# Filler products in the expert stream, a split last load, and a reordered final normalization

## The chip, the cores and the metric

One core of one Trainium2 chip runs the whole program. The metric is the device time of one execution in microseconds; the number for a kernel is the median of several executions. All data is float32.

## What is computed

A transformer block and, behind it, a hybrid layer with a mixture of experts, over 256 tokens of width 1024. The stretch that the change touches is the mixture of experts and the last normalization:

```python
def hier_moe(h, w_group, b_group, w_expert, b_expert, w1, w3, w2):
    ...                                   # each of 256 tokens picks 2 of 32 experts
    def expert_block(args):
        xb, e = args
        hid = jax.nn.silu(xb @ w1[e]) * (xb @ w3[e])
        return hid @ w2[e]
    ...                                   # gated sum back to the tokens

x = x + hier_moe(rms_norm(x, g_ffn), ...)
return rms_norm(x, g_final)               # x * rsqrt(mean(x*x) + eps) * g
```

w1 and w3 are 1024 x 512 and w2 is 512 x 1024 for each of the 32 experts: 2 MiB each, 192 MiB in all.

## The kernel before

The queues of the five engines are written out by hand, with semaphores between them. The dense layers come first (to about 630 us); their weights pass through a ring of three slots and are split into two parts for products in higher precision. Then the experts follow one after another, in quads of four (QUAD = 4). Each expert has 32 slots (SLOTS); products use 32-column tiles of the array, four side by side.

**TensorE**, `quad_body(q)` from L1293: products that gather the quad's tokens (L1305, into banks 4 and 5); then for each expert e: wait for w1, 32 products (L1361, n = 0, into bank 6, columns 0 to 127), wait for w3, 32 products (L1361, n = 1, columns 128 to 255); for e = 0 the gates (`spread_gates`, L1329), else the previous expert's result is added to the tokens' sums (`add_to_tokens`, L1345, banks 0 to 3); wait for w2 and for the turned hidden values, 16 products (L1377, into bank 7, columns 0 to 255). A float32 product shows as two records of stationary load and two of matmul. Quads 0 and 1 are written out (`looped` is false); quads 2 to 7 are one hardware loop (L1387). `keep_warm(n, bank)` (L1058) makes n products of a 128 x 128 tile of ones whose result nobody reads; before, it is used in the program's first microseconds only.

**SyncE** (SP) issues all loads of expert weights. Buffers: `even_w`, `odd_w`, and for the first experts `third_w` and `fourth_w`. `stream(pass_, lo_pair)` (L781) runs over pairs of experts: for each of the three matrices it waits until the matrix of two experts earlier has been used (semaphores e_w1, e_up, e_y) and starts the load (L717), which raises landed_w[parity][which] by 16. Experts 8 to 31 come from this loop. Behind it, four stores of the output, 128 tokens x 512 columns each (L798 to L801); each waits for ScalarE (fin_act) or VectorE (fin_dve).

**ScalarE** applies silu (L1694) and copies an expert's result from bank 7 to `y_part` (L1699); at the end it squares and sums three of the four pieces of the output (L1710) and scales two by the inverse root (L1718).

**VectorE** multiplies silu by the up product (L2336) and turns it (L2341). At the end: a copy and a square sum of the fourth piece (L2366, L2368); `last_mean(tb)` for a block of 128 tokens (L2373 to L2375); two pieces times the gain (L2382); two pieces times inverse root and gain (L2388). **GpSimd** raises the mean to the power -0.5 for block 1, then block 0 (L872).

If more than 32 tokens choose one expert, further passes repeat the stream; with these inputs there is one pass (32 executions of L1694).

Of the kernel before, what the change touches and what calls it, by code (L numbers as in the profile page):

```python
# [31 lines left out]
P = 128  # L32
# [9 lines left out]
UC = 256  # L42
# [6 lines left out]
EXPERTS = GROUPS * PER_GROUP  # L49
# [3 lines left out]
QUAD = 4  # L53
# [236 lines left out]
def layers_kernel(nc, a, table, windows, out):  # L290
# [41 lines left out]
    ones = ones_r[:, :].bitcast(F32)  # L332
# [125 lines left out]
    ps = nc.alloc_psum_tensor("ps", [P, 8, 512], F32)  # L458
# [39 lines left out]
    def sem(name):  # L498
        return nc.alloc_semaphore(name)
# [52 lines left out]
    hot_ready, xg_done, xg_ready, gt_done, gt_ready = (sem(n) for n in ("hot_ready", "xg_done", "xg_ready",  # L552
                                                                        "gt_done", "gt_ready"))
    e_w1, e_w1_half = sem("e_w1"), sem("e_w1_half")
    e_up, e_silu, e_hid, e_hidT, e_y, e_yA = (sem(n) for n in (
        "e_up", "e_silu", "e_hid", "e_hidT", "e_y", "e_y_act"))
    gt_rest, xg_half = sem("gt_rest"), sem("xg_half")
# [111 lines left out]
    def _(sp):  # L669
# [45 lines left out]
        def expert_load(e, places, which, landing):  # L715
            src = sources[which][:, bass.ds(e, 1), :, :].rearrange("p e c n -> p (e c) n")
            sp.dma_start(places[which], src).then_inc(landing, 16)  # L717
# [60 lines left out]
            sp.wait_ge((e_w1, e_up, e_y)[which], 6)  # L778
            expert_load(7, odd_w, which, landed_w[1][which])

        def stream(pass_, lo_pair):  # L781

            with sp.Fori(lo_pair, EXPERTS // 2) as i:
                for odd in range(2):
                    e = sp.snap(i * 2 + odd)
                    used = sp.snap(i * 2 + (pass_ * EXPERTS + odd - 1))
                    for which in range(3):
                        sp.wait_ge((e_w1, e_up, e_y)[which], used)
                        expert_load(e, (even_w, odd_w)[odd], which, landed_w[odd][which])

        stream(0, 4)
        sp.wait_ge(passes_ready, 1)
        n_pass = sp.value_load(passes_i[0:1, 0:1], min_val=1, max_val=T // SLOTS)
        with sp.If(n_pass > 1):
            with sp.Fori(1, n_pass) as again:
                stream(again, 0)
            sp.nop()
        for tb, i in ((1, 0), (1, 1), (0, 0), (0, 1)):  # L798
            sp.wait_ge((fin_act, fin_dve)[i], 2 - tb)
            cols = slice(512 * i, 512 * i + 512)  # L800
            sp.dma_start(out[0, P * tb:P * tb + P, cols], n3[:, tb, cols]).then_inc(fin_out, 16)  # L801
# [75 lines left out]
    def _(pe):  # L877
# [177 lines left out]
                last = mm(ps[:, (6, 6, 7, 2)[n], P * tb:P * tb + P], scale, ident, start=True, stop=True)  # L1055
            last.then_inc(row_done, 1)

        def keep_warm(n, bank):  # L1058

            for _ in range(n):  # L1060
                mm(ps[:, bank, 0:P], ones, ones, start=True, stop=True)

        def turn_block(src, g, tb, n=None):

# [112 lines left out]
        for step, *arg in plan:  # L1177
# [110 lines left out]
           stop=False)  # L1288
# [4 lines left out]
        def quad_body(q):  # L1293

            looped = not isinstance(q, int)
            e0 = pe.snap(q * QUAD) if looped else q * QUAD

            if not looped:
                pe.wait_ge(n3_ready, 2)
            for half in range(2):  # L1300
                for tb in range(TB):
                    if half == 0:
                        pe.wait_ge(hot_part, q * 2 + (tb + 1))
                    for i in range(4):
                        last = mm(ps[:, 4 + half, P * i:P * i + P], n3g[:, tb, 4 * half + i, :], one_hot[:, tb, :],  # L1305
                                  start=tb == 0 and i == 0, stop=tb == 1 and i == 3)
                if half == 0:
                    last.then_inc(xg_half, 1)
            last.then_inc(xg_done, 1)

            def place_of(e):

                if looped:
                    arrived = pe.snap(q * 32 + 8 * (e - 2 + e % 2)) if e % 2 == 0 else pe.snap(q * 32 + 8 * (e - 1))
                    return (even_w, odd_w)[e % 2], landed_w[e % 2], arrived
                if q == 0:
                    return ((even_w, odd_w, third_w, fourth_w)[e],
                            (landed_w[0], landed_w[1], in_third3, in_fourth)[e], 16)
                return ((even_w, odd_w, third_w, odd_w)[e],
                        (landed_w[0], landed_w[1], in_third3, landed_w[1])[e], (32, 32, 32, 48)[e])  # L1320

            def spread_gates():

                pe.wait_ge(hot_ready, q + 1)
                for e in range(QUAD):
                    for tb in range(TB):
                        at_e = T * (e % 2) + P * tb
                        for g in range(4):
                            last = mm(ps[SLOTS * g:SLOTS * g + SLOTS, 4 + e // 2, at_e:at_e + P],  # L1329
                                      gated_hot[:, tb, SLOTS * e:SLOTS * e + SLOTS], ident, start=True, stop=True,  # L1330
                                      tile_position=(0, SLOTS * g))
                last.then_inc(gt_done, 1)

            def add_to_tokens(e):

                if e == 0:
                    pe.wait_ge(gt_ready, q + 1)
                    pe.wait_ge(gt_rest, q + 1)
                    if not looped and q == 0:
                        pe.wait_ge(seeded, 4)  # L1340
                pe.wait_ge(e_yA, pe.snap(e0 + (e + 1)) if looped else e0 + e + 1)
                for tb in range(TB):
                    for g in range(4):
                        part = slice(SLOTS * g, SLOTS * g + SLOTS)
                        last = mm(ps[:, g, T * tb:T * tb + T], gate_T[part, e, P * tb:P * tb + P],  # L1345
                                  y_part[part, e % 2, :], start=False, stop=True, tile_position=(SLOTS * g, 0),
                                  skip_group_check=True)
                last.then_inc(comb_done, 1)

            for e in range(QUAD):  # L1350
                places, landing, arrived = place_of(e)
                done = pe.snap(e0 + e) if looped else e0 + e
                for n in range(2):
                    if not looped and e == 0 and (q == 0 or n == 0):
                        pe.wait_ge(first_half[n], 16 * (q + 1))
                    pe.wait_ge(landing[n], arrived)
                    for c in range(KC):
                        if e == 0 and n == 0 and c % 4 == 0:
                            pe.wait_ge((xg_part, xg_ready)[c // 4], q + 1)
                        for g in range(4):  # L1360
                            last = mm(ps[SLOTS * g:SLOTS * g + SLOTS, 6, P * n:P * n + P],  # L1361
                                      xg[:, c, SLOTS * e:SLOTS * e + SLOTS], places[n][:, c, P * g:P * g + P],
                                      start=c == 0, stop=c == KC - 1, tile_position=(0, SLOTS * g))
                        if not looped and q == 0 and e == 0 and n == 0 and c == KC // 2 - 1:
                            last.then_inc(e_w1_half, 1)
                    last.then_inc((e_w1, e_up)[n], 1)
                if e == 0:
                    spread_gates()
                else:
                    add_to_tokens(e - 1)  # L1370
                if not looped and q == 0 and e == 0:
                    pe.wait_ge(first_half[2], 16)
                pe.wait_ge(landing[2], arrived)
                pe.wait_ge(e_hidT, done + 1)
                for b in range(4):
                    for g in range(4):
                        last = mm(ps[SLOTS * g:SLOTS * g + SLOTS, 7, 0:UC],  # L1377
                                  hid_T[:, SLOTS * b:SLOTS * b + SLOTS], places[2][:, b, UC * g:UC * g + UC],
                                  start=b == 0, stop=b == 3, tile_position=(0, SLOTS * g))
                last.then_inc(e_y, 1)  # L1380
            add_to_tokens(QUAD - 1)
# [340 lines left out]
    def _(dve):  # L1722
# [636 lines left out]
        def piece_of(tb, i):  # L2359

            cols = slice(512 * i, 512 * i + 512)
            return (n3[:, tb, cols].rearrange("p (a b) -> p a b", a=2), ps[:, 2 * i:2 * i + 2, T * tb:T * tb + T],
                    gain_rows[1][:, cols].rearrange("p (a b) -> p a b", a=2))
# [7 lines left out]
        def last_mean(tb):  # L2371

            link(v.tensor_reduce(stat[:, last_event, tb:tb + 1], sq_part[:, tb, 0:2], AX.X, ALU.add))  # L2373
            v.tensor_scalar(stat[:, last_event, 2 + tb:3 + tb], stat[:, last_event, tb:tb + 1], 1.0 / D, EPS, ALU.mult,
                            ALU.add).then_inc(mean_last, 1)  # L2375
# [2 lines left out]
        last_mean(1)  # L2378
        dve.wait_ge(sq_last, 2)
        for tb in (1, 0):  # L2380
            dst, src, gain = piece_of(tb, 0)
            v.tensor_tensor(dst, src, gain, ALU.mult).then_inc(fin_gain, 1)  # L2382
        dve.wait_ge(sq_last, 3)
        last_mean(0)
        for n, tb in enumerate((1, 0)):
            dst, src, gain = piece_of(tb, 1)
            dve.wait_ge(root_last, n + 1)
# [29 lines left out]
```

## Time and profile before

| | |
|---|---|
| median of 3 executions | 1073.48 us (1072.98 to 1074.26) |
| profiled execution, device time | 1076.11 us |
| its span, first to last instruction | 1073.7 us |
| TensorE busy | 932.4 us (87%) |
| VectorE, ScalarE, GpSimd busy | 505.3, 364.0, 29.5 us |
| DMA moved | 310.00 MB, 289 GB/s over the span |
| chain that ended last | TensorE 61%, DMA 34% |

```profile
PE 932.4 (87%) x9984; PEld 767.4 (71%) x9984; DVE 505.3 (47%) x815; ACT 364.0 (34%) x517; POOL 29.5 (3%) x35
```

Busy time is time in which an engine executes; a span is cut into 40 slices on the page, each with the busy share in tenths, the granted clock of TensorE (PEclk; 9 stands for 0.9 or more of 2.4 GHz) and the share of the 16 DMA engines. PE is TensorE's matmuls, PEld its loads of the stationary operand. Behind an instruction stands the idle time before it, and what ended it; "issue" means that the profile shows nothing that was waited for.

### The profile page before, as it was taken

What the parts mean: (1) busy time and instruction counts of PE and PEld (TensorE: products, weight loads), DVE (VectorE), ACT (ScalarE), POOL (GpSimd) and SP (SyncE); (2) the same over time, 40 slices, a digit from 0 to 9 for tenths busy, and PEclk for the clock granted to TensorE, in tenths of its full rate; (3) what the DMA queues carried; (4) which work ended last, traced back from release to release, by engine and by line L of the source; (5) the groups of instructions that cost most, each with busy time, mean ns of one, the idle gap of its engine ahead of it and who ended that gap; (6) DMA issues with size and microseconds to landing.
All of it is one profiled execution on the core that took longest, in us unless ns stands there. A gap on an engine that the chain in (4) does not pass through costs nothing.

```text
span 1073.7 us, 22635 instructions
## 1 busy us (share of the span) xinstructions
PE 932.4 (87%) x9984; PEld 767.4 (71%) x9984; DVE 505.3 (47%) x815; ACT 364.0 (34%) x517; POOL 29.5 (3%) x35
## 2 busy tenths in 40 slices
PE   9999999999999999999999998976766667575764
PEld 8998877888888888988777886754545545364642
DVE  5647768687676668889877651110000101010101
ACT  6445766454444345444666330110000000000001
POOL 0200002110000000000000000000000000000000
PEclk9999999999999999999999999998888889889887
DMA  9954434545554644444457999999999999999994
GB/s 329 312 178 164 152 130 162 172 162 196 195 185 169 214 156 158 158 157 160 156 192 285 397 397 425 419 427 426 427 428 428 428 428 429 428 427 428 429 428 205
DMA packets 86830, 310.00 MB, mean 289 GB/s; under 512 B 5612, under 2 KB 46264, under 8 KB 73976
## 3 DMA queue, kind: packets, MB, share of 16 engines
q1 hardware_dynamic: 85104, 304.72, 72.8%
q0 software_dynamic: 1056, 4.20, 1.2%
q8 instruction: 42, 0.69, 0.3%
q10 hardware_dynamic: 616, 0.28, 0.1%
q14 instruction: 12, 0.10, 0.0%
HBM read 308.15 MB, written 1.05 MB: 288 GB/s over the span
## 4 chain that ended last, share of the span: by engine, by line
PE 61%; DMA 34%; DVE 2%; issue 1%; ACT 1%; POOL 1%; POOLq 0%; SPq 0%; DVEq 0%; ACTq 0%
DMA arena<-in_w 33%; PE ps L882 13%; PE ps L884 12%; PE ps L883 12%; PE ps L1006 7%; PE ps L1377 4%; PE ps L1008 4%; PE ps L1361 2%; DMA arena<-in_w_in 1%; PE ps L1155 1%; PE ps L1143 1%; PE ps L1305 1%; POOL stat L816 0%; PE ps L1067 0%; PE ps L981 0%
## 5 line engine op out<-in xcount | busy, mean ns | idle before, releaser
L1361 PE MATMUL ps<-arena,xg 128*32 128x128 f32 x2816 | 110.7, 322 | 73.6 <-DMA arena<-in_w 72.5
L1747 DVE TENSOR_TENSOR w_split<-arena,w_split 128x2048 fp32r<-128x2048 f32 (+1 forms) x69 | 157.2, 2288 | 29.1 <-ACT w_split L1422 28.6
L2336 DVE TENSOR_TENSOR hid<-silu_e,ps 128x128 f32<-128x128 f32 x32 | 12.1, 378 | 318.5 <-ACT silu_e L1694 318.5
L1361 PEld LDWEIGHTS ps<-arena,xg 128*32 128x32 f32 x2816 | 94.7, 130 | 93.1 <-DMA arena<-in_w 87.2
L1422 ACT ACTIVATE w_split<-arena 128x2048 fp32r<-128x2048 f32 x70 | 132.8, 1900 | 67.7 <-PE ps L884 57.8
L1006 PE MATMUL ps<-x_both,w_split 128*128 128x512 f32 x352 | 124.5, 398 | 0.0
L882 PE MATMUL ps<-w_split,x_both 128*128 128x512 f32 x256 | 102.0, 398 | 0.0
L883 PE MATMUL ps<-w_split,x_both 128*128 128x512 f32 x256 | 99.8, 390 | 0.0
L884 PE MATMUL ps<-w_split,x_both 128*128 128x512 f32 x256 | 99.8, 390 | 0.0
L1008 PE MATMUL ps<-x_both,w_split 128*128 128x256 f32 x352 | 98.6, 280 | 0.0
L1377 PE MATMUL ps<-arena,hid_T 128*32 128x256 f32 x960 | 67.3, 425 | 28.7 <-DMA arena<-in_w 28.1
L1694 ACT ACTIVATE silu_e<-ps 128x128 f32<-128x128 f32 x32 | 8.9, 277 | 243.0 <-PE ps L1361 243.0
L1006 PEld LDWEIGHTS ps<-x_both,w_split 128*128 128x128 f32 x352 | 66.1, 188 | 16.3 <-issue 0.3
L882 PE MATMUL ps<-x_both,w_split 128*128 128x256 f32 (+1 forms) x256 | 72.8, 285 | 0.9 <-ACT p_tok L1450 0.9
L1377 PEld LDWEIGHTS ps<-arena,hid_T 128*32 128x32 f32 x960 | 32.2, 118 | 57.5 <-issue 35.7
L884 PE MATMUL ps<-x_both,w_split 128*128 128x256 f32 (+1 forms) x256 | 72.3, 283 | 0.0
L883 PE MATMUL ps<-x_both,w_split 128*128 128x256 f32 (+1 forms) x256 | 72.3, 282 | 0.0
L882 PE MATMUL ps<-w_split,o_hi 128*128 128x512 f32 (+1 forms) x176 | 68.2, 388 | 0.5 <-DVE gates L1968 0.5
L1757 DVE TENSOR_TENSOR w_split<-arena,w_split 128x2048 fp32r<-128x2048 f32 x24 | 55.0, 2293 | 26.3 <-ACT w_split L1432 25.0
L884 PE MATMUL ps<-w_split,o_lo 128*128 128x512 f32 (+1 forms) x176 | 67.1, 381 | 0.0
L883 PE MATMUL ps<-w_split,o_hi 128*128 128x512 f32 (+1 forms) x176 | 66.9, 380 | 0.0
L1008 PEld LDWEIGHTS ps<-x_both,w_split 128*128 128x128 f32 x352 | 66.4, 189 | 0.3
(328 smaller groups left out, 1470.5 us busy)
## 6 DMA issues: line engine op xcount, KB each, us to landing
arena<-in_w SPq DMA_DIRECT2D x71, 2048.0 KB, 26.2
arena<-in_w_in SPq DMA_DIRECT2D x41, 1024.0 KB, 5.0
even_w<-in_w SPq DMA_DIRECT2D x13, 2048.0 KB, 27.3
arena<-in_w_ffn_in SPq DMA_DIRECT2D x22, 1024.0 KB, 5.1
third_w<-in_w SPq DMA_DIRECT2D x6, 2048.0 KB, 16.1
arena<-in_w_ffn_out SPq DMA_DIRECT2D x11, 1024.0 KB, 4.8
arena<-in_w_out SPq DMA_DIRECT2D x8, 1024.0 KB, 6.1
arena<-in_w SPq DMA_DIRECT2D x6, 1024.0 KB, 6.4
```

The costliest lines, as they stand in the source:

```text
L882: mm(dst, l_hi, r_hi, start=start, stop=False)
L883: mm(dst, l_hi, r_lo, start=False, stop=False)
L884: return mm(dst, l_lo, r_hi, start=False, stop=stop)
L1006: mm(ps[:, bank + n, :], hi[:, c, col], x_both[:, c, :, :].rearrange("p a b -> p (a b)"), start=c == 0, stop=False)
L1008: last = mm(ps[:, bank + n, 0:T], lo[:, c, col], x_hi[:, c, :], start=False, stop=c == kc - 1)
L1143: last = nc.tensor.transpose(m[:, P * t:P * t + P], src[:, P * t:P * t + P], ident)
L1361: last = mm(ps[SLOTS * g:SLOTS * g + SLOTS, 6, P * n:P * n + P], xg[:, c, SLOTS * e:SLOTS * e + SLOTS], places[n][:, c, P * g:P * g + P], ...
L1377: last = mm(ps[SLOTS * g:SLOTS * g + SLOTS, 7, 0:UC], hid_T[:, SLOTS * b:SLOTS * b + SLOTS], places[2][:, b, UC * g:UC * g + UC], start=b ...
L1422: fn(w_hi[:, u % 3, 0:n], ring[:, u % 3, 0:n], ACT.Copy).then_inc(hi_ready, 1)
L1747: v.tensor_tensor(w_lo[:, u % 3, 0:n], ring[:, u % 3, 0:n], w_hi[:, u % 3, 0:n].bitcast(F32), ALU.subtract).then_inc(lo_ready, 1)
L1757: v.tensor_tensor(w_lo[:, s, :], ring[:, s, :], w_hi[:, s, :].bitcast(F32), ALU.subtract)\
L2336: v.tensor_tensor(hid[:, :].rearrange("p (b i) -> p i b", b=4), silu_e[:, :].rearrange("p (i b) -> p i b", b=4), ps[:, 6, P:2 * P].rearran ...
```

## The change

- TensorE: in looped quads, five products of ones ahead of the wait for w1 and five ahead of the wait for w3 (bank 6, columns 256 to 383), three ahead of the wait for w2 (bank 7, the same columns). `keep_warm` takes a column for that.
- SyncE: the stream's loop runs over quads instead of pairs and stops before the last quad, which is written out. The last expert's w2 is loaded by two transfers: rows 0 to 2 of each partition's four (12 KB), which raise landed_w, and row 3 (4 KB), which raises the new semaphore last_block. Each quad of the loop raises last_block by 16 as well.
- TensorE: in each looped quad, before the last quarter (b = 3) of the last expert's down products, a wait for last_block against q * 16 - 16.
- VectorE: the mean of block 0 is computed between the two scalings by the gain instead of behind both.
- SyncE: the stores go in the order block 1 first half, block 0 first half, block 1 second half, block 0 second half.

```diff
--- before.py
+++ after.py
@@ -552,6 +552,7 @@
     hot_ready, xg_done, xg_ready, gt_done, gt_ready = (sem(n) for n in ("hot_ready", "xg_done", "xg_ready",
                                                                         "gt_done", "gt_ready"))
     e_w1, e_w1_half = sem("e_w1"), sem("e_w1_half")
+    last_block = sem("last_block_w2_in")
     e_up, e_silu, e_hid, e_hidT, e_y, e_yA = (sem(n) for n in (
         "e_up", "e_silu", "e_hid", "e_hidT", "e_y", "e_y_act"))
     gt_rest, xg_half = sem("gt_rest"), sem("xg_half")
@@ -778,24 +779,34 @@
             sp.wait_ge((e_w1, e_up, e_y)[which], 6)
             expert_load(7, odd_w, which, landed_w[1][which])
 
-        def stream(pass_, lo_pair):
-
-            with sp.Fori(lo_pair, EXPERTS // 2) as i:
-                for odd in range(2):
-                    e = sp.snap(i * 2 + odd)
-                    used = sp.snap(i * 2 + (pass_ * EXPERTS + odd - 1))
-                    for which in range(3):
-                        sp.wait_ge((e_w1, e_up, e_y)[which], used)
-                        expert_load(e, (even_w, odd_w)[odd], which, landed_w[odd][which])
-
-        stream(0, 4)
+        def stream(pass_, lo_quad):
+
+            def load_expert(e, j, used):
+
+                for which in range(3):
+                    sp.wait_ge((e_w1, e_up, e_y)[which], used)
+                    if isinstance(e, int) and (j, which) == (QUAD - 1, 2):
+                        for rows_, landing in ((slice(0, 3), landed_w[1][2]), (slice(3, 4), last_block)):
+                            sp.dma_start(odd_w[2][:, rows_, :], sources[2][:, e, rows_, :]).then_inc(landing, 16)
+                    else:
+                        expert_load(e, (even_w, odd_w)[j % 2], which, landed_w[j % 2][which])
+
+            with sp.Fori(lo_quad, EXPERTS // QUAD - 1) as i:
+                for j in range(QUAD):
+                    load_expert(sp.snap(i * QUAD + j), j, sp.snap(i * QUAD + (pass_ * EXPERTS + j - 1)))
+                sp.nop().then_inc(last_block, 16)
+            for j in range(QUAD):
+                e = EXPERTS - QUAD + j
+                load_expert(e, j, sp.snap(pass_ * EXPERTS + (e - 1)) if not isinstance(pass_, int) else e - 1)
+
+        stream(0, 2)
         sp.wait_ge(passes_ready, 1)
         n_pass = sp.value_load(passes_i[0:1, 0:1], min_val=1, max_val=T // SLOTS)
         with sp.If(n_pass > 1):
             with sp.Fori(1, n_pass) as again:
                 stream(again, 0)
             sp.nop()
-        for tb, i in ((1, 0), (1, 1), (0, 0), (0, 1)):
+        for tb, i in ((1, 0), (0, 0), (1, 1), (0, 1)):
             sp.wait_ge((fin_act, fin_dve)[i], 2 - tb)
             cols = slice(512 * i, 512 * i + 512)
             sp.dma_start(out[0, P * tb:P * tb + P, cols], n3[:, tb, cols]).then_inc(fin_out, 16)
@@ -1055,10 +1066,10 @@
                 last = mm(ps[:, (6, 6, 7, 2)[n], P * tb:P * tb + P], scale, ident, start=True, stop=True)
             last.then_inc(row_done, 1)
 
-        def keep_warm(n, bank):
+        def keep_warm(n, bank, col=0):
 
             for _ in range(n):
-                mm(ps[:, bank, 0:P], ones, ones, start=True, stop=True)
+                mm(ps[:, bank, col:col + P], ones, ones, start=True, stop=True)
 
         def turn_block(src, g, tb, n=None):
 
@@ -1353,6 +1364,8 @@
                 for n in range(2):
                     if not looped and e == 0 and (q == 0 or n == 0):
                         pe.wait_ge(first_half[n], 16 * (q + 1))
+                    if looped:
+                        keep_warm(5, 6, UC)
                     pe.wait_ge(landing[n], arrived)
                     for c in range(KC):
                         if e == 0 and n == 0 and c % 4 == 0:
@@ -1370,9 +1383,13 @@
                     add_to_tokens(e - 1)
                 if not looped and q == 0 and e == 0:
                     pe.wait_ge(first_half[2], 16)
+                if looped:
+                    keep_warm(3, 7, UC)
                 pe.wait_ge(landing[2], arrived)
                 pe.wait_ge(e_hidT, done + 1)
                 for b in range(4):
+                    if looped and (e, b) == (QUAD - 1, 3):
+                        pe.wait_ge(last_block, pe.snap(q * 16 - 16))
                     for g in range(4):
                         last = mm(ps[SLOTS * g:SLOTS * g + SLOTS, 7, 0:UC],
                                   hid_T[:, SLOTS * b:SLOTS * b + SLOTS], places[2][:, b, UC * g:UC * g + UC],
@@ -2378,10 +2395,11 @@
         last_mean(1)
         dve.wait_ge(sq_last, 2)
         for tb in (1, 0):
+            if not tb:
+                dve.wait_ge(sq_last, 3)
+                last_mean(0)
             dst, src, gain = piece_of(tb, 0)
             v.tensor_tensor(dst, src, gain, ALU.mult).then_inc(fin_gain, 1)
-        dve.wait_ge(sq_last, 3)
-        last_mean(0)
         for n, tb in enumerate((1, 0)):
             dst, src, gain = piece_of(tb, 1)
             dve.wait_ge(root_last, n + 1)
```

## Rows read from the trace of the kernel before

**Rows 1.** The page: span, and granted clock and DMA share in 40 slices.
```profile
span 1073.7 us, 22635 instructions
...
PEclk9999999999999999999999999998888889889887
DMA  9954434545554644444457999999999999999994
```

**Rows 2.** DMA queues and issues, 770 to 1064 us: packets, MB, share; KB each, us to landing.
```profile
q1 hardware_dynamic: 8462, 123.11, 98.4%
issues: line engine op xcount, KB each, median us to landing
arena<-in_w SPq DMA_DIRECT2D x46, 2048.0 KB, 27.2
```

**Rows 3.** Timeline of TensorE, down products of experts 9 to 11: start, us, count, idle before.
```profile
736.39 3.40 PE L1377 MATMUL ps<-arena,hid_T 128*32 128x256 f32 x32 [1.94 <-DMA arena<-in_w]
751.08 1.93 PE L1377 MATMUL ps<-arena,hid_T 128*32 128x256 f32 x32 [0.32 <-DMA arena<-in_w]
...
766.89 3.20 PE L1377 MATMUL ps<-arena,hid_T 128*32 128x256 f32 x32 [1.94 <-DMA arena<-in_w]
```

**Rows 4.** Timeline of the last expert on TensorE.
```profile
1050.71 3.60 PE L1361 MATMUL ps<-arena,xg 128*32 128x128 f32 x64 [2.90 <-DMA arena<-in_w]
...
1055.60 1.95 PE L1361 MATMUL ps<-arena,xg 128*32 128x128 f32 x64 [1.29 <-DMA arena<-in_w]
...
1057.48 1.15 PE L1345 MATMUL ps<-y_part,gate_T 32*128 32x256 f32 x16
...
1060.53 3.28 PE L1377 MATMUL ps<-arena,hid_T 128*32 128x256 f32 x32 [1.90 <-DMA arena<-in_w]
```

**Rows 5.** Stretches: length, busy us (records) of PE, PEld, DVE, ACT, POOL, clock, DMA, GB/s.
```profile
1056.00:1057.00 1.00, 1.00 (x48) 1.00 (x40) 0.00 (x0) 0.00 (x0) 0.00 (x0) 1.00 0.69 295
1057.00:1058.00 1.00, 1.00 (x29) 0.79 (x24) 0.07 (x1) 0.28 (x1) 0.00 (x0) 1.00 0.42 180
...
1059.00:1060.00 1.00, 0.00 (x0) 0.00 (x0) 0.00 (x0) 0.00 (x0) 0.00 (x0) 1.00 0.08 33
```

**Rows 6.** Timeline of TensorE, 0 to 40 us, the products of ones.
```profile
1.07 4.21 PE L1061 MATMUL ps<-ones 128*128 128x128 f32 x18 [1.07 <-DVE ones L2074]
...
6.72 1.95 PE L1061 MATMUL ps<-ones 128*128 128x128 f32 x16
```

**Rows 7.** Timeline of the end, VectorE and GpSimd.
```profile
1067.24 1.28 DVE L2382 TENSOR_TENSOR n<-ps,gain_row 128x512 f32<-128x512 f32 x2
1067.42 0.57 POOL L872 TENSOR_TENSOR stat<-stat,minus_half 128x1 f32<-128x1 f32 x1 [402.38 <-DVE stat L2374]
...
1068.62 0.15 DVE L2374 TENSOR_SCALAR stat<-stat 128x1 f32<-128x1 f32 x1
1068.69 0.74 DVE L2388 SCALAR_TENSOR_TENSOR n<-n,stat,gain_row 128x512 f32<-128x512 f32 x1
...
1068.85 1.00 POOL L872 TENSOR_TENSOR stat<-stat,minus_half 128x1 f32<-128x1 f32 x1 [0.86 <-DVE stat L2374]
...
1069.88 0.75 DVE L2388 SCALAR_TENSOR_TENSOR n<-ps,stat,gain_row 128x512 f32<-128x512 f32 x1 [0.45 <-POOL stat L872]
```

**Rows 8.** Timeline of SyncE, the last two stores of the output.
```profile
1070.63 0.33 SPq L801 DMA_DIRECT2D out<-n  x1
...
1071.01 0.43 SPq L801 DMA_DIRECT2D out<-n  x1
```

**Rows 9.** Stretches as in rows 5: between two stalls, loop start to a stall, one quad.
```profile
649.25:655.26 6.01, 5.38 (x128) 4.09 (x127) 0.00 (x0) 0.39 (x1) 0.00 (x0) 1.00 1.02 431
710.17:720.40 10.23, 8.54 (x191) 7.84 (x188) 1.38 (x3) 0.87 (x2) 0.00 (x0) 1.00 1.01 426
771.75:829.15 57.40, 38.26 (x804) 29.51 (x800) 5.21 (x14) 3.83 (x10) 0.00 (x0) 0.88 1.01 428
```

**Rows 10.** DMA queue of instruction fetches, 640 to 702 us, then 709 to 770 us.
```profile
q8 instruction: 10, 0.16, 1.0%
...
q8 instruction: 7, 0.11, 0.8%
```

## The prediction

> **What bounds the kernel now.** I began with the page's slices: from about 590 us on the DMA row stands at 9 in every slice to the last, while PEclk drops below full speed [rows 1]. Next the DMA view of 770 to 1064 us: 2048 KB loads alone, each landing some 27 us after its issue [rows 2]. Down products that wait for a load start 14.69 us apart (736.39, 751.08) [rows 3], which is three loads, so a load takes 4.90 us and more than five are in flight. TensorE is idle in between; what it wins inside the stream is worth nothing. Only three things count: when the last bytes land, what follows them, and anything else that uses the 16 DMA engines.
>
> At the end, expert 31's up matrix is used from 1055.60, its last down matrix from 1060.53, after 1.90 us of idleness [rows 4]. The DMA share falls from 0.69 over 0.42 to 0.08 in 1056 to 1060 [rows 5]: the engines end one after another, and the slowest sets the landing. Behind it stands a serial chain to the end.
>
> **Part 1: last down matrix in two transfers, dummies ahead.** The profiled run computed this matrix in 3.28 us [rows 4]; the same 32 records take 1.93 us at 2.4 GHz (751.08), 3.40 at nearly 1.2 GHz throughout [rows 3].
> - Transfer: three quarters of the bytes land a quarter of 4.90 us, 1.22 us, earlier. Bounds: nothing earlier (if both completions come together) to 1.22. I take 1.2; the quarters queue behind each other on the same engines. A second set of packet starts I take as 0.1 us at most.
> - Dummies: 18 records ran in 4.21 us cold, 16 in 1.95 us warm [rows 6]. One dummy is two records, so 0.24 us warm, 0.47 cold: five are 1.2 or 2.3 us, three 0.7 or 1.4 us. In the stream they lie in idle time of 2.90 us (1050.71) and 1.90 us (1060.53) [rows 4]; where a quad begins they make TensorE some 1 us late, which the 27 us of loads in flight cover [rows 2]. If that cover were gone, each would cost its own time.
> - Clock: the longest regular idle stretch shrinks from 2.90 to 1.7 us. Since the up products and additions (1055.60 to 1058.63) are followed directly by dummies, I expect 2.4 GHz at the last matrix.
> - New end: additions end 1058.63 [rows 4], three dummies to 1059.37, just behind the first landing. Three quarters of 1.93 us to 1060.82; the last quarter has landed at about 1060.6, its products take 0.48: 1061.30, against 1060.53 + 3.28 = 1063.81. **-2.5 us**; if cold in spite of the dummies, 1063.4 (-0.4). Against an execution whose last matrix ran warm already (end 1062.46) it is only -1.2.
>
> **Part 2: the mean ahead of the second scaling, stores.** Before: two scalings from 1067.24, 0.60 us apart, then the mean (ends 1068.77), then the second power 1068.85 to 1069.85, then the last products at 1069.88 [rows 7]. After: scaling one, mean from 1067.84 to about 1068.2, scaling two beside the power. The first power took 0.57, the second 1.00 us, beside L2388, which reads two SBUF tensors [rows 7]. Moved, the power runs beside L2382, which reads one from PSUM; I take 0.57, so the root is there at 1068.85. L2388 then runs back to back (1068.69, 1069.43) and ends at 1070.2 instead of 1070.63. The store of block 0's first half goes at about 1069.7, and the other two follow 0.38 us apart, the spacing of the last two now (1070.63, 1071.01) [rows 8]: the last at 1070.45 instead of 1071.01. **-0.6 us**, 0 to -0.6. If the power stays at 1.00 the gain is about 0.2. The Trainium skill, SBUF — State Buffer, section Who interferes with whom, says that a VectorE instruction with two SBUF inputs contends with a GpSimd instruction that reads SBUF; by it the 0.57 stands, and the two rows agree.
>
> The nops and the unrolled last quad on SP, and the wait on last_block, cost 0: SP only has to issue within those 27 us. Behind that wait are the 8 last records alone, which need these bytes anyway.
>
> **Part 3: what else the dummies bring, code.** Each dummy is 4 instructions (two loads of the stationary operand, two products), 52 per quad: 208. A quad of the loop now has 804 + 800 records, with branches and register work about 1612 [rows 9]. Instruction fetches are packets of 16 KB: 10 are 0.16 MB, and 7 fell in the first looped quad, 709 to 770 [rows 10]; from 770 on there is none, the DMA view has no line for them [rows 2]. So the first pass brings the body in and five passes reuse it. A block holds 256 instructions: TensorE stalls for "issue" at 649.25 and again at 655.27, 255 records apart [rows 9]. Such a stall also lies 377 instructions behind the loop's start (720.4 [rows 9]), so the body starts 121 before a block's end: 121 + 5 x 256 + 211 = 1612, **seven blocks**. Seven fetches were seen, six for the rest and one for the block behind the loop. Eight blocks stayed, then. After: 121 + 6 x 256 + 163 = 1820, **eight blocks**, and the next makes nine. No row shows nine kept. If the store holds eight, block nine drives out the first, and each block fetched drives out the one wanted next: 9 x 5 + 1 = 46 more fetches.
> - Bytes: 46 x 16 KB = 0.75 MB at 428 GB/s [rows 2], 1.8 us if the engines share it evenly. Upper bound: between 751.08 and 766.89 three loads took 15.81 instead of 14.69 us [rows 3]; 1.12 us over the 7 fetches of that quad is 0.16 each, 7.4 us for 46. The slowest engine counts, not the mean, but over 46 fetches it evens out; I take **+2.2 us**, near the lower end.
> - TensorE's stalls: 10 fetches in the dense stretch of 640 to 702 us [rows 10] are one per 6.2 us; nine blocks at that pace are 56 us of a quad's 58.7, so TensorE barely catches up; covered by the loads in flight.
> The Trainium skill, Runtime: NRT & Kernel Launch, section Instruction fetch mechanics, gives TensorE's instruction store as 128 KiB, a FIFO refilled in 16 KiB blocks, eight of them. By it this case comes true; the trace shows only that eight are kept.
>
> **Sum.** Against the profiled execution's own 1076.11 us: -2.5 - 0.6 + 2.2 = -0.9, 1075.2 us. That execution lies 2.6 us above the median of 1073.48. Its 24 looped experts have six slow down products (2.9 us or more; two of them, 736.39 and 766.89, are in [rows 3]), and the 24th, the last, is one. So I give the median execution a warm last matrix with 3 in 4. Against the median I therefore use -1.2 for part 1: -1.2 - 0.6 + 2.2 = +0.4, **1073.9 us**.
>
> **Rivals.**
> - A, forecast (0.45): whole body refetched, 1073.9, own range 1072.5 to 1076.5. For: the body needs one block more than was ever seen kept. Against: the limit itself is in no row.
> - B (0.30): nine blocks are kept. Then part 3 is 0: 1073.48 - 1.8 = 1071.7, down to 1070.4 if the median execution was cold at the end like the profiled one (-3.1). For: five passes without a fetch [rows 2].
> - C (0.10): the ninth block and the first displace only each other, 2 fetches a pass, 11 in all, 0.4 to 1.8 us: 1072.4.
> - D, slower (0.08): the refetches fall on the engines that land last, or TensorE falls behind the loads. At 0.16 us each: 1073.48 - 1.8 + 7.4 = 1079.1. It decides from (1.8 + 2.15) / 46 = 0.086 us per fetch.
> - E (0.07): the change doesn't do what it says. The clock is low at the last matrix, or both transfers complete together: part 1 is +1.0 against a warm median (end 1063.4 against 1062.46) and, without refetches, 1073.48 + 1.0 - 0.6 = 1073.9.
>
> **Chances.** This kernel's measurement tells about 0.2% from no change, 2.15 us: faster is below 1071.3, slower above 1075.6. Faster: 0.4 of B, a fifth of C, a twentieth of A, with some margin 0.18. Slower: D and 0.15 of A, 0.16. Same: 0.66. Range: B's low end nearly whole, A's high end and a little of D: 1070.8 to 1077.0.
>
> **What would show it.** The last matrix: products in two groups, 24 records from about 1.1 us before the other 8, all at the 60 ns pace of 1.93/32. PEclk at 9 in the stream. Fetches: a line "instruction" in the DMA view of a later looped quad, about 9 per quad (A, D), 2 (C), none (B); with them stalls for "issue" at the quad's start. The span between two down products a quad apart: 58.7 us now, more by 0.4 a quad in A. Tail: second power 0.57 us beside L2382's successor, three stores 0.38 us apart. I am wrong if there are fetches and no longer stream, or a cold last matrix.

## The result, and the profile after

The changed kernel takes 1080.38 us (median of 4, 1080.06 to 1081.32) against 1073.33 us (median of 4) for the kernel before: ratio 1.006, 95% interval 1.0048 to 1.0072. It is slower by 7.05 us, and by 3.4 us outside the predicted range. Its profiled execution took 1080.06 us with a span of 1078.2 us.

The page of the kernel after: span, granted clock and DMA share, and the queue of instruction fetches. That queue had 42 packets before.

```profile
span 1078.2 us, 23858 instructions
...
PEclk9999999999999999999999999999899899989899
DMA  9954434546555644455448999999999999999995
...
q8 instruction: 88, 1.44, 0.5%
```

88 against 42 is 46 more: 9 x 5 + 1, the number of the prediction. The DMA view of 770 to 1070 us (packets, MB, share) has 45 of them, where [rows 2] had none, and the loads land after 23 us instead of 27:

```profile
q1 hardware_dynamic: 8569, 122.56, 96.5%
q8 instruction: 45, 0.74, 1.0%
...
arena<-in_w SPq DMA_DIRECT2D x44, 2048.0 KB, 23.2
```

TensorE's waits of the same stretch (us in total, times, longest), and one of the five in the timeline, at the start of a quad:

```profile
PE ps L1316 <- issue: 26.3, 5, 5.5
...
896.35 5.20 PE L1316 MATMUL ps<-one_hot,n3g 128*128 128x128 f32 x32 [5.12 <-issue]
```

Five loop passes, five stalls of some 5 us ahead of the first product of a quad. The profile names no engine or load that TensorE waited for; that the first block of the body is not there is the reading which the experiments test. The stalls themselves are caught up within the quad, since by its last expert TensorE waits for loads again. The up matrix of that expert, five quads in a row (timeline of TensorE):

```profile
821.29 1.95 PE L1374 MATMUL ps<-arena,xg 128*32 128x128 f32 x64 [2.04 <-DMA arena<-in_w]
...
882.18 3.59 PE L1374 MATMUL ps<-arena,xg 128*32 128x128 f32 x64 [2.29 <-DMA arena<-in_w]
...
942.41 1.95 PE L1374 MATMUL ps<-arena,xg 128*32 128x128 f32 x64 [1.64 <-DMA arena<-in_w]
...
1002.66 1.95 PE L1374 MATMUL ps<-arena,xg 128*32 128x128 f32 x64 [1.64 <-DMA arena<-in_w]
...
1062.82 1.95 PE L1374 MATMUL ps<-arena,xg 128*32 128x128 f32 x64 [1.59 <-DMA arena<-in_w]
```

All five wait for a landing, and the four steps between them are 60.89, 60.23, 60.25 and 60.16 us. Before, three loads took 14.69 us [rows 3], twelve 58.76. So a pass with nine fetches lengthens the stream by 1.4 to 2.1 us.

One stretch inside the stream, then its end (length, busy us of PE, PEld, DVE, ACT, POOL, clock, DMA share, GB/s):

```profile
1025.00:1028.00 3.00, 3.00 (x78) 2.68 (x73) 0.00 (x0) 0.00 (x0) 0.00 (x0) 1.00 0.78 289
1056.00:1060.00 4.00, 3.41 (x79) 3.02 (x76) 0.00 (x0) 0.38 (x1) 0.00 (x0) 1.00 0.69 290
1060.00:1064.00 4.00, 2.41 (x54) 2.22 (x58) 0.00 (x0) 0.00 (x0) 0.00 (x0) 1.00 0.49 204
1064.00:1068.00 4.00, 4.00 (x79) 2.82 (x74) 0.69 (x2) 0.28 (x1) 0.00 (x0) 1.00 0.29 116
```

From 1060 to 1064 us only half of the DMA engines' time is used, while the last loads are still on their way. Before, the share of 1056 to 1060 us was 0.37 and then nothing. So the engines no longer end together, and the late ones set the landing.

The end of the kernel after (timeline: TensorE, VectorE, GpSimd, then the first and the last two stores on SyncE):

```profile
1064.70 1.15 PE L1356 MATMUL ps<-y_part,gate_T 32*128 32x256 f32 x16
...
1065.77 0.94 PE L1072 MATMUL ps<-ones 128*128 128x128 f32 x6
...
1066.64 1.93 PE L1394 MATMUL ps<-arena,hid_T 128*32 128x256 f32 x32
...
1070.29 0.69 DVE L2383 COPY n<-ps 128x512 f32<-128x512 f32 x1 [4.42 <-PE ps L1356]
...
1073.02 0.56 POOL L883 TENSOR_TENSOR stat<-stat,minus_half 128x1 f32<-128x1 f32 x1 [0.27 <-DVE stat L2391]
1073.45 0.74 DVE L2406 SCALAR_TENSOR_TENSOR n<-n,stat,gain_row 128x512 f32<-128x512 f32 x1
...
1074.11 0.74 DVE L2406 SCALAR_TENSOR_TENSOR n<-ps,stat,gain_row 128x512 f32<-128x512 f32 x1
...
1073.58 0.35 SPq L812 DMA_DIRECT2D out<-n  x1
...
1074.76 0.94 SPq L812 DMA_DIRECT2D out<-n  x2
```

The last matrix runs warm (1.93 us) directly behind the dummies. Its three quarters landed at 1066.44 us, 1.24 us before the last one, and TensorE began at 1066.64, so all four quarters ran without a break: the two separate groups that were forecast do not show, because the last quarter was there before its turn. The second power takes 0.56 us and the last two products follow each other (compare [rows 4, 7]).

The trace's landing times close the sum. The last bytes land at 1067.68 us instead of 1060.41: **+7.27**. From there to VectorE's copy there are 2.61 us instead of 5.12: **-2.51**. From the copy to the landing of the last store are 7.50 instead of 7.83: **-0.33**. That is +4.43; the spans differ by 4.5.

### The profile page after: what moved, and what is told of

Its sections match the earlier page's. It is cut to its first block, busy times and chain, and to the rows that moved or that the text cites. A ratio compares the mean times of both kernels' runs of the same rounds, so it can differ in the third digit from the quotient of the medians.

```text
span 1078.2 us, 23858 instructions
## 1 busy us (share of the span) xinstructions
PE 989.0 (92%) x10608; PEld 826.2 (77%) x10608; DVE 505.0 (47%) x815; ACT 364.1 (34%) x517; POOL 29.0 (3%) x35
## 3 DMA queue, kind: packets, MB, share of 16 engines
q0 software_dynamic: 1056, 4.20, 1.2%
## 4 chain that ended last, share of the span: by engine, by line
PE 73%; DMA 18%; issue 4%; DVE 2%; ACT 1%; POOL 0%; SPq 0%; DVEq 0%; ACTq 0%
DMA arena<-in_w 17%; PE ps L893 13%; PE ps L895 12%; PE ps L894 12%; PE ps L1017 7%; PE ps L1374 7%; PE ps L1394 4%; PE ps L1019 4%; PE ps L1316 3%; PE ps L1072 3%; PE ps L1356 1%; DMA arena<-in_w_in 1%; PE ps L1340 1%; PE ps L1166 1%; PE ps L1154 1%
## 5 line engine op out<-in xcount | busy, mean ns | idle before, releaser
L1374 PE MATMUL ps<-arena,xg 128*32 128x128 f32 x2816 | 88.7, 277 | 25.4 <-DMA arena<-in_w 20.7
L1072 PEld LDWEIGHTS ps<-ones 128*128 128x128 f32 x710 | 87.2, 195 | 20.5 <-issue 19.3
L1072 PE MATMUL ps<-ones 128*128 128x128 f32 x710 | 101.0, 289 | 1.1 <-DVE ones L2091 1.1
L1374 PEld LDWEIGHTS ps<-arena,xg 128*32 128x32 f32 x2816 | 76.2, 111 | 32.9 <-DMA arena<-in_w 23.3
L1017 PEld LDWEIGHTS ps<-x_both,w_split 128*128 128x128 f32 x352 | 66.2, 188 | 16.4 <-issue 0.3
L1394 PE MATMUL ps<-arena,hid_T 128*32 128x256 f32 x960 | 58.6, 382 | 10.3 <-DMA arena<-in_w 9.3
```

The costliest lines, as they stand in the source:

```text
L1017: mm(ps[:, bank + n, :], hi[:, c, col], x_both[:, c, :, :].rearrange("p a b -> p (a b)"), start=c == 0, stop=False)
L1072: mm(ps[:, bank, col:col + P], ones, ones, start=True, stop=True)
L1394: last = mm(ps[SLOTS * g:SLOTS * g + SLOTS, 7, 0:UC], hid_T[:, SLOTS * b:SLOTS * b + SLOTS], places[2][:, b, UC * g:UC * g + UC], start=b ...
```

## Experiments

The theory after the result: 52 dummies are 208 instructions, these carry the loop's body from seven to eight blocks, and with the next block nine are wanted; the refetch of all nine in each pass delays the landings. The rivals: the dummies' work on TensorE does it; SyncE's new loop and the split load do it; and, for the size, the bytes of the refetch count, or the engine on which they fall.

**All but the dummies.** `keep_warm(5, 6, UC)` and `keep_warm(3, 7, UC)` are taken out of the changed kernel:

```diff
-                    if looped:
-                        keep_warm(5, 6, UC)
...
-                if looped:
-                    keep_warm(3, 7, UC)
```

> All of the change but the dummies: a quad has 1613 instructions instead of 1821 and spans seven blocks of 256. Theory (the dummies' code costs the refetch): no instruction fetch after the first looped quad, loads 4.90 us apart, so last bytes at 1060.4 us of the span as before; the split and the moved mean remain, with the clock left to chance: 0.6 to 1.8 us under the kernel before. Rival 1 (the dummies' work, not their code): no fetch difference would be seen and the time would also be back near 1072, so this run only sizes the sum. Rival 2 (the split load or the unrolled last quad on SyncE costs the 7 us): the time stays at 1078 to 1081.

1072.53 us against 1074.06 us, ratio 0.9984 (0.9974 to 0.9993): faster by 1.5 us by the medians, 1.7 by the ratio. 42 fetches. Split load, unrolled quad and moved mean together cost nothing; they gain about what the prediction gave them against a warm median (-1.2 and -0.6). This is the lowest median of all runs, with the ten dummies below within its noise.

**The dummies alone**, in the kernel before.

```diff
+                    if looped:
+                        keep_warm(5, 6, UC)
                     pe.wait_ge(landing[n], arrived)
...
+                if looped:
+                    keep_warm(3, 7, UC)
                 pe.wait_ge(landing[2], arrived)
```

> The kernel before with the 52 dummies per looped quad and nothing else: 1820 instructions. Code theory: 46 fetches more than before, stream 7.2 us longer, a warm last matrix saves up to 1.35: 6 to 8 us slower than before, 1079.5 to 1081.5. Rival (part of the 7 us belongs to the split load or to SyncE's unrolled quad): less than 5 us slower.

1082.64 against 1074.40 us, ratio 1.0073 (1.0057 to 1.0089), 88 fetches. The last bytes land at 1067.62 us, 7.2 us later than before. So the dummies alone bring the whole delay of the stream, and no other part is needed for it.

**Ten and thirteen dummies**, all in the quad's last expert: 12 instructions apart, on both sides of the block's end.

```diff
-                    if looped:
-                        keep_warm(5, 6, UC)
+                    if looped and e == QUAD - 1:
+                        keep_warm((3, 4)[n], 6, UC)
...
-                if looped:
+                if looped and e == QUAD - 1:
                     keep_warm(3, 7, UC)
```

> As the change, but only 10 dummies per looped quad, all in its last expert (3, 4 and 3): 1653 instructions, which by the count (121 + 6 x 256 = 1657) still fit seven blocks. Code theory: no fetch from the second looped quad on, 1.5 to 3 us under the kernel before. Rival (each dummy costs by its work on TensorE, in proportion): 10 of 52 dummies cost 7.2 x 10/52 = 1.4 us, as does the neighbour with 13 within 0.4.

With ten: 1072.80 against 1074.06 us, ratio 0.9990 (0.9979 to 1.0000), 42 fetches.

The other kernel has `(5, 5)[n]` in that place.

> As the run with ten, but 13 dummies in the last expert of each looped quad (5, 5 and 3): 1665 instructions, 8 past the seventh block. Code theory: about 9 fetches per quad, 40 to 46 in all after the first looped quad, and the stream 5 to 8 us longer than with ten, for three dummies more. Rival (work): within 0.4 us of the run with ten, no fetches.

With thirteen: 1074.98 us, ratio 1.0007 (0.9992 to 1.0022), single executions from 1072.0 to 1080.0. The threshold lies where the count put it, but the size was wrong: 52 fetches, not 88. The DMA views of 775 to 944 us and of 944 to 1003 us show where they fell (packets, MB, share; the first stretch has no line for instructions):

```profile
q1 hardware_dynamic: 4972, 72.35, 100.6%
...
q1 hardware_dynamic: 1708, 24.84, 99.5%
q8 instruction: 9, 0.15, 1.2%
```

Three passes without a fetch, then one with all nine (the last pass has none again). By the count, the body reaches only some 8 instructions into its eighth block before it branches back, and mostly the next block is then not asked for. So eight blocks of body do stay, if the count is right; it is the ninth that starts the exchange, and then all nine are fetched. Whether it starts differs between passes, and in all likelihood between executions, which fits the wide spread. The last bytes landed at 1062.52 us, 1.9 later than with ten, for these nine fetches.

**The kernel before, its loop only shifted**: no instruction is added to the loop.

```diff
+        keep_warm(16, 6)
         with pe.Fori(2, n_pass * (EXPERTS // QUAD)) as q:
```

> The kernel before, with 16 dummies (64 instructions) once, ahead of TensorE's loop; the loop's body is untouched at 1612 instructions but starts 57 instead of 121 before a block's end and so spans eight blocks. Code theory: fetches in every looped quad, 5 to 8 us slower than before though no instruction was added to the loop. Rival (dummies inside the loop cost by work, or by colliding with the landings): 16 dummies once, 3.9 us of TensorE time in a stretch with 27 us of loads in flight: within 0.3 us of before.

1076.34 against 1074.06 us, ratio 1.0015 (1.0003 to 1.0027), executions from 1073.5 to 1078.5; 52 fetches, ten more than before. In the profiled execution one pass, 1003 to 1062 us, had nine:

```profile
q8 instruction: 9, 0.15, 1.1%
```

Position alone brings the refetch, here too in one pass of five, as the body goes only some 15 to 20 instructions into the eighth block. The expected 5 to 8 us were too much for the same reason as with thirteen. The last bytes landed at 1062.06 us, 1.65 later than before. In both kernels the DMA share, read in stretches of 3 us, stayed at 0.96 or more through the pass with the fetches: the engines never lacked loads there, so loads asked for too late do not explain this delay.

**Forty dummies, aligned and not.** The same loop body (40 dummies per quad: 2 and 2, 3 and 5, 4 and 4, 4 and 4 ahead of w1 and w3, 3 ahead of w2), with and without 33 dummies ahead of the loop.

```diff
-                        keep_warm(5, 6, UC)
+                        keep_warm(((2, 2), (3, 5), (4, 4), (4, 4))[e][n], 6, UC)
...
+        keep_warm(33, 6)
         with pe.Fori(2, n_pass * (EXPERTS // QUAD)) as q:
```

> As the change, but 40 dummies per looped quad instead of 52, and 33 dummies (132 instructions) once ahead of the loop, so that the body of 1773 instructions starts 3 to 11 instructions into a block and fits seven blocks. Theory (code): no fetch after the first looped quad, the stream as long as before, 1.5 to 3 us under the kernel before, although TensorE does 77% of the added work. Rival (the dummies' work delays TensorE and through it the loads): 0.77 of the change's 7 us, 1078 to 1080.

1073.40 against 1074.36 us, ratio 0.9992 (0.9980 to 1.0003). The page of this kernel:

```profile
PEclk9999999999999999999999999989999999999998
...
q8 instruction: 43, 0.70, 0.3%
```

> The run with 40 dummies, its 33 dummies ahead of the loop taken away and nothing else: the same body of 1773 instructions now starts some 125 before a block's end and spans eight blocks, over 100 instructions into the eighth. Code theory: about 9 fetches in each looped quad again and 5 to 8 us more than with the 33, though the program is shorter. Rival (the 40 dummies are below some amount of work that matters): as fast as with the 33, within 0.5 us.

Without the 33: 1081.53 against 1074.40 us, ratio 1.0064 (1.0047 to 1.0082), 88 fetches. In its waits the stall at the quad's start is back, 27.2 us in five:

```profile
PE ps L1316 <- issue: 27.2, 5, 5.6
```

This pair decides between code and work. The loop is the same to the last instruction, the faster program is the longer one, and some 8 us (by the medians; each was measured against its own executions of the kernel before) go with 132 instructions of position. It also shows what the dummies are worth: a clock at 2.4 GHz in nearly the whole stream, and no more time gained than without dummies.

**Thin dummies**, 8 columns instead of 128.

```diff
-                mm(ps[:, bank, col:col + P], ones, ones, start=True, stop=True)
+                n_cols = 8 if col else P
+                mm(ps[:, bank, col:col + n_cols], ones, ones[:, 0:n_cols], start=True, stop=True)
```

> As the change, all 52 dummies per quad, but each moves 8 columns instead of 128: the same 1821 instructions with about a fifth of the matmul time. Code theory: 9 fetches in each looped quad as in the change, 88 in all, and the same time within 1.5 us (1079 to 1082). Rival (work): near the kernel before, 1072 to 1074, whatever the fetches.

1082.28 against 1074.36 us, ratio 1.0080 (1.0060 to 1.0101), 88 fetches. This run does not tell the theories apart: the dummies' busy time fell from 71.5 to 65.7 us only, and not to a fifth as expected. These are the groups of products of ones, 770 to 1060 us, in this kernel and in the one with the dummies alone:

```profile
L1073 PE MATMUL ps<-ones 128*128 128x8 f32 x495 | 65.7, 260 | 0.0
...
L1061 PE MATMUL ps<-ones 128*128 128x128 f32 x505 | 71.5, 286 | 0.0
```

**What a 16 KB packet costs.** The kernel before with extra loads on ScalarE's queue behind each copy of an expert's result, 16 KB per expert, into a dead buffer: in one kernel as four packets on one DMA engine, in the other as one load over all 16 (`gain_rows[0][0:16, 0:256]`).

```diff
+                if not isinstance(q, int):
+                    for p in range(4):
+                        act.dma_start(gain_rows[0][p:p + 1, 0:1021], a["x"][0][p:p + 1, 0:1021]).then_inc(extra_in, 16)
+                    act.wait_ge(extra_in, act.snap(q * 256 + (64 * (e + 1) - 256)))
```

> The kernel before, with four more loads of 4084 bytes (an odd number of elements, so that each is one packet on one DMA engine) per expert from the fifth on, on ScalarE's queue, into a buffer no longer used: 28 x 16 KB, less than the 46 x 16 KB of refetched code. Theory (the slowest engine sets every landing, so a 16 KB packet costs its whole 0.6 us where it falls on that engine): 28 x 0.6 = 17 us longer, less the engine's lead of at most 4 us: 12 to 17 us. Rival (bytes count, 0.46 MB over all engines): 1.1 us.

1088.55 against 1074.36 us, ratio 1.0135 (1.0118 to 1.0152): +14.2 us, 0.51 for each of the 28 times 16 KB. The last weights land at 1074.37 us, 13.96 later than before.

> As the run with one engine, the same bytes per expert in one load of 16 partitions x 1 KB, a packet for each engine. Both theories expect about the bytes' share, 28 x 0.05 = 1.3 us; if this run is as slow as the one with one engine, the extra transfers cost by their number or through ScalarE's wait, not by the engine on which they fall.

1080.31 us, ratio 1.0053 (1.0035 to 1.0071): +5.9 us, 0.21 per 16 KB; the last weights land at 1066.57 us, 6.16 later. By their bytes 1.3 us were expected; why it is more stays open. The DMA views of both, 775 to 1060 us (one engine, then all engines):

```profile
q1 hardware_dynamic: 8326, 121.23, 100.1%
q10 hardware_dynamic: 152, 0.31, 0.3%
...
q1 hardware_dynamic: 8263, 120.34, 100.2%
q10 hardware_dynamic: 624, 0.32, 0.4%
```

0.31 MB in this stretch is a quarter of a percent of the bytes; the loads' own share stays at 100%. Yet the kernel with one engine loses 1.3%. Its last stretches show how (as above):

```profile
1056.00:1060.00 4.00, 3.68 (x52) 2.29 (x48) 0.69 (x2) 0.28 (x1) 0.00 (x0) 0.66 0.90 385
1060.00:1064.00 4.00, 1.19 (x24) 0.46 (x16) 0.00 (x0) 0.38 (x1) 0.00 (x0) 1.00 0.06 25
1064.00:1068.00 4.00, 1.96 (x64) 1.69 (x64) 0.00 (x0) 0.00 (x0) 0.00 (x0) 1.00 0.07 28
1068.00:1072.00 4.00, 2.46 (x48) 2.28 (x52) 0.00 (x0) 0.00 (x0) 0.00 (x0) 0.62 0.06 26
```

A share of 0.06 is one engine of 16: fifteen are done at about 1060 us, as before, and one alone works for 14 us more. A load needs all its engines, so the slowest decides, and what the others gain in advance is lost at the end. ScalarE's wait for the extra loads is not the cause, since the loads kept the engines busy until then. In the changed kernel the share of 0.49 after 1060 us is that of about half of the engines still at work; the view gives only the mean over all 16.

Of the refetch: a 16 KB packet at a sixteenth of 428 GB/s takes 0.6 us, so nine of them spread evenly over 16 engines would be 9 x 0.6 / 16 = 0.34 us per pass; measured are 1.4 to 2.1. The fetches' own records are longer: 45 packets fill 1.0% of 16 engines' 300 us, 1.1 us each, and spread evenly that would still be 0.6 us per pass only. With 0.5 to 0.6 us for each packet on the deciding engine, two to four of the nine fall there, with 1.1 us one or two. That is worked out, not seen: the trace doesn't name the engines, and which engine a block's fetch takes stays open.

**The moved mean and stores alone.** The stores go in the order of the changed kernel.

```diff
+            if not tb:
+                dve.wait_ge(sq_last, 3)
+                last_mean(0)
             dst, src, gain = piece_of(tb, 0)
...
-        dve.wait_ge(sq_last, 3)
-        last_mean(0)
```

> The kernel before with the mean of block 0 ahead of the second scaling and the new order of the stores, nothing else. Theory: second power at 0.57 us instead of 1.00, root 0.8 us earlier, VectorE's last three products back to back, last store 0.5 to 0.6 us earlier. Rival (the power keeps its 1.00 us): 0.2 us.

1074.05 against 1074.40 us, ratio 0.9997 (0.9988 to 1.0006): not told from no change by its time. Its trace shows the mechanism (the power at 0.56 us, the last store issued 4.97 us behind VectorE's copy instead of 5.48) and where two fifths of it go: the last store lands 2.56 us after its issue instead of 2.35, as the stores now stand closer together. Copy to last landing: 7.52 instead of 7.83 us.

**The split load alone**, without dummies and with the end as before.

```diff
+                    if isinstance(e, int) and (j, which) == (QUAD - 1, 2):
+                        for rows_, landing in ((slice(0, 3), landed_w[1][2]), (slice(3, 4), last_block)):
+                            sp.dma_start(odd_w[2][:, rows_, :], sources[2][:, e, rows_, :]).then_inc(landing, 16)
```

> The kernel before with the last expert's down matrix in two transfers, SyncE's last quad written out, and TensorE's wait; no dummies, the end as before. Theory: two landings 1.2 us apart, the second where the one was before within 0.1; 24 of 32 records are done by then: 1.1 to 1.3 us faster where the clock is the same. Rival: no gain, because both completions come together, or TensorE, cold without the dummies, takes 2.5 us for three quarters (gain 0.8 then).

The wait for `last_block` on TensorE is in it too. 1073.50 against 1074.40 us, ratio 0.9985 (0.9976 to 0.9994): 0.9 us by the medians, 1.6 by the ratio. The two parts landed at 1059.09 and 1060.33 us, 1.24 apart. The last expert on TensorE:

```profile
1055.47 3.61 PE L1372 MATMUL ps<-arena,xg 128*32 128x128 f32 x64 [2.95 <-DMA arena<-in_w]
1059.01 1.15 PE L1356 MATMUL ps<-y_part,gate_T 32*128 32x256 f32 x16
1060.24 1.93 PE L1390 MATMUL ps<-arena,hid_T 128*32 128x256 f32 x32
```

Here the up matrix ran cold and made TensorE late, so that it could not use the first part before 1060.24, when the second was about to land too. The down products end at 1062.17, only 0.3 us before the 1062.46 of an unsplit matrix that runs warm [rows 3, 4]; against the cold one of the kernel before, most of the gain in this execution is the clock. The expected 24 records ahead of the second landing did not come about.

## Why the prediction was wrong

1. **The bound.** Right: the stream set the time in both kernels. More matmul time moved little by itself: with forty dummies per quad and no refetch the last bytes landed at 1061.32 us, 0.9 later than before, which is within what executions differ by. The stalls of 5 us come only together with the fetches, so no run prices them alone. They are made good by the end of each quad, but the cover was thinner than forecast: between 1025 and 1028 us the DMA share fell to 0.78, after the fifth stall, where it had been at 1.0 before. That in such stretches a part of the 7 us arises is neither shown nor excluded.
2. **Part 1.** Right, -2.5 forecast, -2.51 measured between two profiled executions, of which the one before was cold at the end; landings 1.24 us apart, last matrix warm. Without dummies the last matrix ran warm too in the profiled execution (end 1060.44, last bytes at 1059.59 us), so the dummies only secure the clock. How much the split gives by itself is known to within 0.6 to 2.6 us (the interval of its run).
3. **Part 2.** The mechanism was right (power 0.56 us, products back to back, stores 0.38 and 0.49 us apart), the term too large: -0.6 forecast, -0.33 measured. The issue of the last store did come 0.52 us earlier behind the copy; missing was that it then lands later, after 2.54 us instead of 2.35.
4. **Part 3, the code.** The count was right: seven blocks to eight, the ninth too many, 46 fetches. The Trainium skill, Runtime: NRT & Kernel Launch, section Instruction fetch mechanics, has the same eight blocks for TensorE, and the traces agree: with thirteen dummies eight stayed through three passes, and where a ninth came, all were fetched.
5. **The step that failed is the price of a fetch.** The prediction had two ends, 0.04 us (bytes over all engines) and 0.16 us (landings of the first looped quad [rows 3, 10]), and took 0.048 "near the lower end", because over 46 fetches the engines should even out. They don't: measured are 7.27 / 46 = 0.158 us, +7.27 in place of +2.2, and the DMA share of 0.49 after 1060 us shows the engines ending apart. The two kernels with one refetching pass give 0.18 to 0.21 us per fetch (1.65 and 1.87 us for nine), with the scatter of single executions in it. The upper end was the one row that showed fetches and landings together; the lower was a calculation that assumed an even spread, against the prediction's own sentence that the slowest engine counts. With 0.16 the forecast's sum had been rival D's 1079.1, which stood at 8 in 100.
6. **Against the median.** With measured terms the sum is -1.2 - 0.33 + 7.27 = +5.7 against 7.05 measured. The rest of 1.3 us is not explained; the stream's end of a kernel moves by about 1 us from one profiled execution to another (last bytes at 1059.59 without dummies, 1060.65 with ten), and the 7.27 is itself a difference of two such executions.
7. **Chances.** "Same" stood at 0.66 because A was priced at +0.4. The mechanism was the likeliest case and came true, its price put it outside the range.

## What to carry over

Count the instructions of a long hardware loop on each engine, with the position at which it starts: a filler instruction that costs no time in an idle gap still costs code, and at the edge of the instruction store a few of them, or a shift of the loop, decide whether the whole body is fetched again in each pass. Where a transfer stream sets the time, price any other traffic by the slowest DMA engine, from a row that shows it beside the landings, not by its share of the bytes. And take a term's price from the row that shows the event itself, even where a calculation gives a friendlier one.

## What the runs showed of the hardware

- By the count from the stalls, a loop body in eight blocks of 256 instructions stays in TensorE's store as long as the block behind it isn't asked for. With some 8 to 20 instructions in the last block before the branch it was asked for in one pass of five (two kernels, 52 fetches each), with over 100 in all five (four kernels, 88 each).
- A pass with refetch began with a stall of TensorE, 5.1 to 5.5 us in the changed kernel, 7.0 in the one such pass with thirteen dummies, while the DMA engines were full.
- 16 KB over all 16 engines from a second queue, 1 KB each, cost 0.21 us of the stream per transfer, about five times their bytes' time (16 KB at 428 GB/s are 0.04 us); the same bytes on one engine cost 0.51, and that engine then worked 14 us alone.
- Dummies of 8 columns kept TensorE busy nearly as long as those of 128: 65.7 against 71.5 us for about 500 records, 260 against 286 ns per record.
- Four stores issued within 1.7 us land after 2.05, 2.05, 2.35 and 2.54 us.
